# The 32 sample rows as weights in four column quarters, and the channel panels over 512 tokens twice

## The chip, the cores and the metric

The kernel runs on one core of a Trainium2 chip. The time is the device time of one launch in microseconds (us); the median of three timed runs of the kernel before is 4745.81 us (4744.82 to 4746.95). The profile is one further execution. The engines are named as in the profile: PE is TensorE's matmuls and PEld its weight loads, DVE is VectorE, ACT is ScalarE, POOL is GpSimd, SP is SyncE, which here only issues DMAs.

## The reference, cut to what matters

One step of a hybrid encoder layer for 1024 prompt frames and 32 sample frames: a combined input projection, differential attention, a causal convolution and a grouped state-space scan, output products, a retrieval over 16384 experts, and a gated per-layer embedding. The change lies in the combined projection, which is computed for both groups of frames with the same weights:

```python
h = rms_norm(x, lp['norm_mix_g'])
q, k, v, z, xbc, dt_raw, gates = jnp.split(h @ lp['w_in'], SPLIT_AT, axis=-1)
```

`h` is 1056 x 1024 here (1024 prompt rows, then 32 sample rows), and `w_in` is 1024 x 10272. All inputs are float32.

## The kernel before

`project_convolve_scan` is the first stage; attention and the retrieval follow it, each behind a barrier. It keeps h transposed on chip, so that the 1024 model channels lie on the partitions in 8 slices of 128. To get close to float32 from the faster `fp32r` matmuls, h and the weights are each held as a leading part and a rest, and `product` (line 94) makes three matmuls for each of the 8 slices: 24 in one unit of work. A matmul on plain float32 operands is issued as two instructions (two passes); the profile counts these.

The columns of `w_in` are cut into 27 panels: panel 0 is 512 columns of q; panels 1 to 6 are the 3072 channels of x, B and C ("xbc"); 7 to 10 are z; 11 and 12 are v; then 14 half panels of 256 columns follow, 6 of q and k and 8 of the gates. The panels of q, k, xbc and gates are "by channel": a block of 128 weight columns is the stationary operand, and the 1056 tokens stream in three units of `TS` = 352. There are 56 such blocks (4, then 24, then 28). The panels of z and v are "by token": 128 tokens are stationary and 512 weight columns stream; each has 9 units, and the ninth holds the 32 sample rows. After panel 0 comes the step size "dt" (32 columns), for 9 token tiles of 24 matmuls each.

What sets the order is written out by hand, and all engines are in program order:

- POOL loads panel p into the single raw buffer `wp` (`load`, line 310), which is free once DVE has split panel p-1. In POOL's own program the load of panel p+1 stands behind `keep_tail` and `put_past` (lines 323 and 315) for the four blocks of panel p-1, and the last of these waits until DVE has convolved the last block but one buffer ago.
- DVE splits a panel into lead and rest (lines 89 and 91), then convolves the four blocks of the panel before (lines 554 and 557). In the front part it scales and splits the transposed tiles of h and the four quarters of panel 0 (`scale`, `rest`, `first_panel`).
- PE computes the units into PSUM banks, six before the half panels and three (`NBS`) in them, and transposes each convolved block after the third unit of the next (line 937), when ACT has activated it (line 796).
- ACT moves each unit out of PSUM (line 767, and 784 for xbc), into one of four staging buffers, which SP stores.
- Beside the half panels the scan runs in 36 steps. Before each even unit PE does the step's sums (lines 1010 to 1012), before each odd one the products of the step before (1029 and 1030); DVE, ACT and POOL work between them. Three steps stand beside each half panel of six units. The steps' state rows are written out beside the first and the last of them.

## Time and profile before

| | |
|---|---|
| median of the timed runs | 4745.81 us |
| time of the profiled execution | 4760.91 us |
| its span | 4759.3 us |
| PE busy | 3775.6 us, 79% of the span |
| DVE busy | 2834.1 us, 60% |
| ACT busy | 1627.9 us, 34% |
| POOL busy | 1464.9 us, 31% |
| mean granted TensorE clock | 0.897 |
| the 24 matmuls of all `product` units at 128x352 into the low banks (lines 99 to 101) | 359.0, 329.4 and 329.0 us busy |

The span is from the first to the last instruction of the profiled execution; the time of that execution is 1.6 us more, and it lies 15 us above the median of the timed runs. Busy times of PE count each matmul from its start to its end, and matmuls overlap, so a matmul's cost is read from the distance between two starts. The first stage ends at about 1280 us. The granted clock is given as a share of 2.4 GHz.

### The profile page before, as it was taken

The numbers are of one execution on the slowest core, as the hardware profiler recorded it, in microseconds if no ns is written. First come the engines' busy times: TensorE is split into PE (matmuls) and PEld (weight loads), VectorE is DVE, ScalarE is ACT, GpSimd is POOL, SyncE is SP. The second block draws the span as 40 slices with busy tenths as digits, with TensorE's granted clock in tenths as the row PEclk, the third lists the DMA queues.
The fourth block names the chain that finished last, engine by engine and source line by source line (L and its number), as shares of the span: only waits on it lengthen the run. The fifth ranks groups of instructions, "written<-read, shape, count | busy, mean of one in ns | idle before, by whom it ended". The sixth has DMA issues, their size and how long they took to land.

```text
span 4759.3 us, 53107 instructions
## 1 busy us (share of the span) xinstructions
PE 3775.6 (79%) x17205; PEld 2215.6 (47%) x17205; DVE 2834.1 (60%) x6237; ACT 1627.9 (34%) x4726; POOL 1464.9 (31%) x1391
## 2 busy tenths in 40 slices
PE   8999999999899888867777878656765766666658
PEld 8999777888766674334232334311311212212212
DVE  3444113666377537666557666666766666666774
ACT  2222111234266302333333333334444344444433
POOL 1100002222111003334334444344444444444442
PEclk8999999999899999998888999877887878978879
DMA  2223222344323359999999999999999999999996
GB/s 93 74 84 124 88 90 73 125 129 129 110 81 102 109 184 373 403 402 395 387 377 380 408 405 419 420 419 416 411 419 407 407 419 411 399 421 418 416 404 266
DMA packets 310588, 1379.97 MB, mean 290 GB/s; under 512 B 37840, under 2 KB 112320, under 8 KB 175168
## 3 DMA queue, kind: packets, MB, share of 16 engines
q0 software_dynamic: 167728, 1166.48, 60.6%
q1 hardware_dynamic: 142608, 210.36, 12.7%
q8 instruction: 130, 2.13, 0.2%
q14 instruction: 122, 1.00, 0.1%
HBM read 1295.71 MB, written 81.01 MB: 289 GB/s over the span
## 4 chain that ended last, share of the span: by engine, by line
DMA 29%; PE 20%; DVE 7%; issue 4%; POOL 4%; ACT 2%; ACTq 0%; DVEq 0%; POOLq 0%
DMA peer_uv<-in_peer_uv_dram,peer_idx 29%; PE peer_acc L2762 10%; PE peer_fo L2701 4%; POOL peer_uv L1872 3%; DVE peer_uv L2018 3%; PE peer_fo L2714 2%; PE peer_fo L2601 2%; PE peer_tb L2545 1%; ACT peer_scaled L2336 1%; DVE peer_hot L1979 0%; DVE peer_hot L1982 0%; DVE peer_sel L1985 0%; ACT peer_ge L2331 0%; PE peer_acc L2650 0%; PE peer_fo L2619 0%
## 5 line engine op out<-in xcount | busy, mean ns | idle before, releaser
L2762 PE MATMUL peer_acc<-peer_uv,peer_scaled 128*64 128x512 f32 (+1 forms) x4224 | 1298.7, 734 | 699.3 <-ACT peer_scaled L2336 676.6
L2018 DVE CUSTOM_DVE_ANT_0 peer_uv<-peer_uv,peer_rep 128x1024 f32<-128x1024 f32 x1056 | 1282.8, 1224 | 938.0 <-DMA peer_uv<-in_peer_uv_dram,peer_idx 894.2
L1872 POOL DMA_INDIRECT peer_uv<-in_peer_uv_dram,peer_idx x1056 | 1217.6, 1153 | 1722.3 <-PE peer_acc L2762 1472.7
L2762 PEld LDWEIGHTS peer_acc<-peer_uv,peer_scaled 128*64 128x64 f32 (+1 forms) x4224 | 310.0, 158 | 1528.6 <-ACT peer_scaled L2336 953.4
L2331 ACT ACTIVATE peer_ge<-peer_pre 128x1 f32<-128x1 f32 x1056 | 213.4, 202 | 1678.3 <-DVE peer_pre L2018 1631.0
L2701 PE MATMUL peer_fo<-peer_space 128*128 128x256 f32 (+2 forms) x1152 | 407.4, 496 | 101.5 <-DVE peer_space L2072 44.1
L2336 ACT ACTIVATE peer_scaled<-peer_eased,peer_ge 128x64 f32<-128x64 f32 (+1 forms) x1056 | 366.4, 347 | 122.0 <-ACT peer_ge L2331 2.4
L99 PE MATMUL proj_bank<-proj_hTh,proj_wplead 128*128 128x352 f32 x1008 | 359.0, 356 | 1.8 <-DVE proj_wprest L91 1.8
L2329 ACT ACTIVATE peer_eased<-peer_fold,peer_gw 128x64 f32<-128x64 f32 (+1 forms) x1056 | 351.1, 332 | 1.1 <-DVE peer_gw L2000 1.1
L2701 PEld LDWEIGHTS peer_fo<-peer_space 128*128 128x128 f32 x1152 | 217.3, 201 | 285.9 <-issue 234.6
L100 PE MATMUL proj_bank<-proj_hTr,proj_wplead 128*128 128x352 f32 x1008 | 329.4, 327 | 0.0
L101 PE MATMUL proj_bank<-proj_hTh,proj_wprest 128*128 128x352 f32 x1008 | 329.0, 326 | 0.0
L767 ACT ACTIVATE proj_stg<-proj_bank 128x352 f32<-128x352 f32 (+2 forms) x117 | 57.7, 495 | 490.0 <-PE proj_bank L101 490.0
L99 PEld LDWEIGHTS proj_bank<-proj_hTh,proj_wplead 128*128 128x128 f32 x1008 | 193.7, 192 | 25.1 <-issue 22.2
L100 PEld LDWEIGHTS proj_bank<-proj_hTr,proj_wplead 128*128 128x128 f32 x1008 | 193.6, 192 | 15.9 <-issue 15.9
L101 PEld LDWEIGHTS proj_bank<-proj_hTh,proj_wprest 128*128 128x128 f32 x1008 | 193.1, 192 | 0.0
L89 DVE CAST proj_wplead<-proj_wp 128x4096 fp32r<-128x4096 f32 (+2 forms) x17 | 31.5, 1852 | 261.1 <-DMA proj_wp<-in_w_in_dram 126.4
L2714 PE MATMUL peer_fo<-peer_space 128*128 128x128 f32 (+1 forms) x1152 | 151.0, 287 | 38.6 <-DVE peer_space L2082 18.8
L2714 PEld LDWEIGHTS peer_fo<-peer_space 128*128 128x128 f32 (+1 forms) x1152 | 138.1, 189 | 85.3 <-issue 80.4
L2545 PEld LDWEIGHTS peer_tb<-peer_hT,peer_wq 128*128 128x128 f32 x1152 | 142.2, 202 | 69.3 <-issue 66.4
L2545 PE MATMUL peer_tb<-peer_hT,peer_wq 128*128 128x128 f32 x1152 | 155.0, 291 | 1.4 <-ACT peer_hT L2294 1.4
L1234 DVE CUSTOM_DVE_ANT_0 attn_e<-attn_S,bias_negdist 128x128 f32<-128x128 f32 (+5 forms) x144 | 103.1, 750 | 60.4 <-PE attn_S L1361 52.4
(376 smaller groups left out, 5460.6 us busy)
## 6 DMA issues: line engine op xcount, KB each, us to landing
proj_wp<-in_w_in_dram POOLq DMA_DIRECT2D x13, 2048.0 KB, 9.6
peer_space<-in_w_ssm_o_dram SPq DMA_DIRECT2D x48, 512.0 KB
peer_uv<-in_peer_uv_dram,peer_idx POOLq DMA_INDIRECT x1056
proj_wp<-in_w_in_dram POOLq DMA_DIRECT2D x14, 1024.0 KB, 7.9
peer_space<-in_w_attn_o_dram SPq DMA_DIRECT2D x24, 512.0 KB
peer_space<-in_w_out_dram SPq DMA_DIRECT2D x24, 512.0 KB
scratch_xtok<-proj_shared SPq DMA_DIRECT2D x20, 512.0 KB, 3.2
scratch_chan<-proj_stg SPq DMA_DIRECT2D x48, 176.0 KB
```

The lines of the kernel that those rows point to most:

```text
L99: pe.matmul(out, a.bitcast(F32R), b.bitcast(F32R), start=(k == 0), stop=False)
L100: pe.matmul(out, a.bitcast(F32R), br.bitcast(F32R), start=False, stop=False)
L101: mm = pe.matmul(out, ar.bitcast(F32R), b.bitcast(F32R), start=False, stop=(k == last))
L1872: pool.indirect_dma_start(uv[k][:], None, io["peer_uv"], bass.IndirectOffsetOnAxis(ap=idx[t % 2][:, col:col + 1], axis=0)).then_inc(uv_in[ ...
L2018: dve.tensor_tensor_reduce(uv[k][:, 0:D], uv[k][:, 0:D], rep[j][:], 1.0, 0.0, ALU.mult, ALU.add, pre[:, k:k + 1]).then_inc(u_done, 1)
L2329: act.activation(eased[n % 2][:, 0:r], fold[:] if r == DEC else fold2[:], ACT.Copy, scale=gw[t % 2][:, col:col + 1]).then_inc(eased_done, 1)
L2331: act.activation(ge[:, k:k + 1], pre[:, k:k + 1], ACT.Gelu_apprx_tanh).then_inc(gelu_done, 1)
L2336: act.activation(scaled[k][:, 0:r], eased[n % 2][:, 0:r], ACT.Copy, scale=ge[:, k:k + 1]).then_inc(scaled_done, 1)
L2545: x = pe.matmul(tb[h // 4][:, h % 4, :], wq[:, k, h * P:(h + 1) * P], hT[:, k, :], start=(k == 0), stop=(k == DK - 1))
L2701: x = pe.matmul(bank[n % 2][:, 0:e], w[q % WR][:, k, :], xb[p % 2][:, k, 0:e], start=(k == 0), stop=(k == CB - 1))
L2714: x = pe.matmul(bank[n % 2][0:r, i * P:(i + 1) * P], sm[:, k, inside(i, r)], w[q % WR][:, k, :], start=(k == 0), stop=(k == CB - 1))
L2762: x = pe.matmul(acc[group(t, slot % groups_of(t)), h:h + HALF], scaled[slot][:, 0:r], uv[slot][:, D + h:D + h + HALF], start=(it == 0 and ...
```

## The change

The 32 sample rows leave the three-matmul units. Their transposed h is kept in a buffer of its own in plain float32 (`own`) and is now the stationary operand, 32 columns wide; the raw float32 panel streams past it. The 8 slices of the contraction are dealt over four column quarters of the array, so that quarter q sums slices q and q+4 in rows 32q to 32q+31 of one PSUM bank (`quarters`). ACT copies the bank to `part`, and a matmul with `fold` (four 32x32 identities on top of each other) adds the four quarters up: by channel it gives 128 channels x 32 tokens with `part` as weights, by token 32 x 512 with `fold` as weights. Panel 0, whose raw buffer is needed early, uses its lead and rest instead. The step size is computed in the same way, with the 32 columns of its weights stationary.

The third unit of a channel block and the ninth of a token panel thus become one float32 matmul each, and the other two units of a channel block cover 512 tokens. In the half panels the two short units now stand behind the four long ones. PSUM gives up a bank for `quarters`, so the bank counts fall to 5 and 2, and the staging buffers to 3. Two waits are added on POOL's loads, since PE now reads the raw panel too. The sample part of panel p+1 stands on PE behind the first unit of panel p.

```diff
-TS = T // NSPLIT
+SEG = 512
...
-    NB, NBS, NST = 6, 3, 4
+    NB, NBS, NST = 5, 2, 3
...
+            blocks = PANELS[p][3] // P
+            order = [(a, b) for a in range(blocks) for b in range(NSPLIT)]
+            if p >= WIDE:
+                order = [x for x in order if x[1] < NSPLIT - 1] + [x for x in order if x[1] == NSPLIT - 1]
+            return [(FIRST[p] + u, a, b) for u, (a, b) in enumerate(order)]
...
+    def third(b):
+
+        return slice(b * SEG, min((b + 1) * SEG, T))
+
+    def third_width(b):
+        return third(b).stop - third(b).start
+
+    def part_at(p):
+
+        return p + NSPLIT if p else 0
...
-        wdth, wdtr = s.sb("wdth", [P, DK, SH]), s.sb("wdtr", [P, DK, SH])
+        own = s.sb("own", [P, DK, DEC])
         stg = [s.sb(f"stg{i}", [P, PANEL]) for i in range(NST)]
+        part, fold = s.sb("part", [P, PANEL]), s.sb("fold", [P, DEC])
...
+                    if p > 1:
+                        pool.wait_ge(part_made, part_at(p - 1 if p <= WIDE else p - 2) + 1)
                     pool.dma_start(raw_of(p), w_cols(col + at, w)).then_inc(panel_in[p % 2], 16)
...
+                dve.tensor_reduce(fold[:], c.ident[:].rearrange("p (q m) -> p m q", m=DEC), AX_X, ALU.add).then_inc(fold_done, 1)
...
+                def evacuate_part(p):
+                    w = PANELS[p][3]
+                    act.wait_ge(part_made, part_at(p) + 1)
+                    act.activation(part[:, 0:w], quarters[:, 0:w], ACT.Copy).then_inc(part_out, 1)
...
                 def evacuate_dt():
+                    for b in range(NSPLIT):
+                        act.wait_ge(part_made, b + 2)
+                        act.activation(part[:, 0:third_width(b)], quarters[:, 0:third_width(b)], ACT.Copy).then_inc(part_out, 1)
...
                 for p in range(1, len(PANELS)):
+                    evacuate_part(p)
                     if PANELS[p][0] != "xbc":
...
+                def sample_part(p):
+
+                    w = PANELS[p][3]
+                    if p:
+                        pe.wait_ge(panel_in[p % 2], 16 * (p // 2 + 1))
+                        pe.wait_ge(part_out, part_at(p))
+                    else:
+                        pe.wait_ge(h_lead, 2 * NT)
+                    terms = [(k, x) for k in range(0, DK, 4) for x in ((raw_of(p),) if p else (lead_of(p), rest_of(p)))]
+                    for i, (k, x) in enumerate(terms):
+                        for q in range(4):
+                            mm = pe.matmul(quarters[q * DEC:(q + 1) * DEC, 0:w], own[:, k + q, :], x[:, k + q, :],
+                                           start=(i == 0), stop=(i == len(terms) - 1))
+                    mm.then_inc(part_made, 1)
+
...
+                    w = third_width(b)
+                    pe.wait_ge(part_out, b + 1)
+                    terms = [(k, x) for k in range(0, DK, 4) for x in ((hTh[:, :, third(b)], hTr[:, :, third(b)]) if b < NSPLIT - 1 else (own[:],))]
+                    for i, (k, x) in enumerate(terms):
+                        for q in range(4):
+                            mm = pe.matmul(quarters[q * SH:(q + 1) * SH, 0:w], wdt[:, k + q, :], x[:, k + q, :],
+                                           start=(i == 0), stop=(i == len(terms) - 1))
+                    mm.then_inc(part_made, 1)
...
-                    if kind in BY_CHANNEL:
-                        cols, toks = slice(a * P, (a + 1) * P), slice(b * TS, (b + 1) * TS)
-                        mm = product(pe, bank[bank_of(n)][:, 0:TS], [(lead[:, k, cols], rest[:, k, cols]) for k in range(DK)],
+                    if kind not in BY_CHANNEL and a == NPT:
+                        pe.wait_ge(part_out, part_at(p) + 1)
+                        mm = pe.matmul(bank[bank_of(n)][0:DEC, :], fold[:], part[:], start=True, stop=True)
+                    elif kind in BY_CHANNEL and b == NSPLIT - 1:
+                        pe.wait_ge(part_out, part_at(p) + 1)
+                        if n < FIRST[1]:
+                            pe.wait_ge(fold_done, 1)
+                        mm = pe.matmul(bank[bank_of(n)][:, 0:DEC], part[:, a * P:(a + 1) * P], fold[:], start=True, stop=True)
+                    elif kind in BY_CHANNEL:
+                        cols, toks = slice(a * P, (a + 1) * P), third(b)
+                        mm = product(pe, bank[bank_of(n)][:, 0:SEG], [(lead[:, k, cols], rest[:, k, cols]) for k in range(DK)],
                                      [(hTh[:, k, toks], hTr[:, k, toks]) for k in range(DK)])
...
-                            pe.wait_ge(h_rest, 2 * 3)
+                            pe.wait_ge(h_rest, 2 * 4)
                     elif i == 4:
-                        pe.wait_ge(h_rest, 2 * 6)
-                    elif i == 8:
-                        pe.wait_ge(h_rest, 2 * NT)
+                        pe.wait_ge(h_rest, 2 * 8)
                     unit(0, n, a, b)
+                    if i == 6:
+                        sample_part(0)
...
-                for t in range(NT):
-                    n = rows_of(t)
-                    here = slice(t * P, t * P + n)
-                    mm = product(pe, bank[DT % NB][0:n, t * SH:(t + 1) * SH], [(hTh[:, k, here], hTr[:, k, here]) for k in range(DK)],
-                                 [(wdth[:, k, :], wdtr[:, k, :]) for k in range(DK)])
+                for b in range(NSPLIT):
+                    step_size_part(b)
+                    pe.wait_ge(part_out, b + 2)
+                    for t in range(4 * b, min(4 * b + 4, NT)):
+                        n, at = rows_of(t), (t - 4 * b) * P
+                        mm = pe.matmul(bank[DT % NB][0:n, t * SH:(t + 1) * SH], part[:, at:at + n], fold[:], start=True, stop=True)
...
+                sample_part(1)
...
                         unit(p, n, a, b)
+                        if i == 0 and p + 1 < len(PANELS):
+                            sample_part(p + 1)
```

Three places show what moves. The first is on PE, at the end of the first unit of panel 2 (`own` holds the sample rows, `wp` the raw panel, `tb` the transposes). Before:

```order
L101 MATMUL proj_bank<-proj_hTh,proj_wprest 128x352
L940 MATMUL proj_tb<-ident,proj_shared 32x128 [waits proj_rows_out]
L99 MATMUL proj_bank<-proj_hTh,proj_wplead 128x352 [waits proj_evac_done]
L100 MATMUL proj_bank<-proj_hTr,proj_wplead 128x352
L101 MATMUL proj_bank<-proj_hTh,proj_wprest 128x352
```

After:

```order
L101 MATMUL proj_bank<-proj_hTh,proj_wprest 128x512
L950 MATMUL proj_quarters<-proj_wp,proj_own 32x512 [waits proj_part_out,proj_panel_in1]
L950 MATMUL proj_quarters<-proj_wp,proj_own 32x512 x7
L1002 MATMUL proj_tb<-ident,proj_shared 32x128 [waits proj_rows_out]
L99 MATMUL proj_bank<-proj_hTh,proj_wplead 128x512 [waits proj_evac_done]
```

Eight float32 matmuls on the raw panel 3 stand between the first and the second unit of panel 2, and with them a wait for that panel's arrival.

The second place is on POOL: the load of panel 3 and what stands ahead of it in POOL's program, the last rows for the blocks of panel 1. Before:

```order
L326 COPY proj_tailr<-proj_shared 128x3
L320 COPY proj_shared<-proj_pastT 128x3 [waits proj_tail_kept,proj_convolved]
L326 COPY proj_tailr<-proj_shared 128x3 [waits proj_evac_done]
L326 COPY proj_tailr<-proj_shared 128x3
L320 COPY proj_shared<-proj_pastT 128x3 [waits proj_tail_kept,proj_convolved]
L313 DMA proj_wp<-in_w_in_dram 128x8x512 [waits proj_w_split]
```

After:

```order
L345 COPY proj_tailr<-proj_shared 128x3
L339 COPY proj_shared<-proj_pastT 128x3 [waits proj_tail_kept,proj_convolved]
L345 COPY proj_tailr<-proj_shared 128x3 [waits proj_evac_done]
L345 COPY proj_tailr<-proj_shared 128x3
L339 COPY proj_shared<-proj_pastT 128x3 [waits proj_tail_kept,proj_convolved]
L332 DMA proj_wp<-in_w_in_dram 128x8x512 [waits proj_part_made,proj_w_split]
```

The load stays where it was, with one wait more.

The third place is on PE in the half panels, at the third scan step of a panel (`scan` and `shared` hold the scan's tables, `seg`, `yh` and `tb` are its PSUM banks). Before, a unit of 24 matmuls follows the sums and another follows the products; one step's sums and the start of that unit are:

```order
L1010 MATMUL proj_seg<-proj_scan,below 128x512
L1011 MATMUL proj_yh<-proj_shared 128x128
L1012 MATMUL proj_tb<-proj_shared 128x512
L99 MATMUL proj_bank<-proj_hTh,proj_wplead 128x352 [waits proj_evac_done]
L100 MATMUL proj_bank<-proj_hTr,proj_wplead 128x352
```

After, from the third step's sums to the next panel's:

```order
L1075 MATMUL proj_seg<-proj_scan,below 128x512
L1076 MATMUL proj_yh<-proj_shared 128x128
L1077 MATMUL proj_tb<-proj_shared 128x512
L978 MATMUL proj_bank<-proj_fold,proj_part 128x32 [waits proj_part_out,proj_evac_done]
L1094 MATMUL proj_tb<-proj_scan 128x64 [waits proj_y_step,proj_cbm_done,proj_sadd_done,proj_wx_done,proj_out_done,proj_dtx_done,proj_M_done]
L1094 MATMUL proj_tb<-proj_scan 128x64 x7
L1095 MATMUL proj_yh<-proj_scan,proj_shared 128x512
L978 MATMUL proj_bank<-proj_fold,proj_part 128x32 [waits proj_part_out,proj_evac_done]
L1075 MATMUL proj_seg<-proj_scan,below 128x512 [waits proj_exp_done,proj_carried_done,proj_ld_in0,proj_sadd_done,proj_R_done,proj_w_split]
```

Between these sums and products, and between these products and the next sums, one matmul stands where 24 stood.

## Rows read from the trace of the kernel before

**Rows 1.** The profile page: busy time of each engine, share of the span, instructions.
```profile
PE 3775.6 (79%) x17205; PEld 2215.6 (47%) x17205; DVE 2834.1 (60%) x6237; ACT 1627.9 (34%) x4726; POOL 1464.9 (31%) x1391
```

**Rows 2.** Windows: stretch, its us, busy us of each engine, PEclk, DMA share, GB/s.
```profile
81.45:120.19 38.74, 38.74 (x218) 38.74 (x216) 0.00 (x0) 0.47 (x1) 0.00 (x0) 0.55 0.01 5
170.44:395.52 225.08, 209.27 (x1300) 206.88 (x1298) 103.33 (x73) 58.81 (x129) 18.04 (x53) 0.95 0.26 84
```

**Rows 3.** Timeline of PE: start us, us, engine, line, op; first matmuls of units.
```profile
58.41 0.32 PE L99 MATMUL proj_bank<-proj_hTh,proj_wplead 128*128 128x352 f32 x1
62.25 0.32 PE L99 MATMUL proj_bank<-proj_hTh,proj_wplead 128*128 128x352 f32 x1
...
557.95 0.39 PE L99 MATMUL proj_seg<-proj_wplead,proj_hTh 128*128 128x512 f32 x1
...
561.44 0.39 PE L99 MATMUL proj_seg<-proj_wplead,proj_hTh 128*128 128x512 f32 x1
```

**Rows 4.** Timeline of PE in the scan: products of one step, first matmuls after them.
```profile
1002.26 0.73 PE L99 MATMUL proj_bank<-proj_hTh,proj_wplead 128*128 128x352 f32 x1
...
1013.15 1.89 PE L1029 MATMUL proj_tb<-proj_scan 128*128 128x64 f32 x16
...
1015.39 0.73 PE L99 MATMUL proj_bank<-proj_hTh,proj_wplead 128*128 128x352 f32 x1
```

**Rows 5.** Timeline of PE in the retrieval: eight passes in two column halves, then in one quarter.
```profile
3114.62 1.94 PE L2762 MATMUL peer_acc<-peer_uv,peer_scaled 128*64 128x512 f32 x8 [1.52 <-ACT peer_scaled L2336]
...
4698.81 3.62 PE L2762 MATMUL peer_acc<-peer_uv,peer_scaled 128*32 128x512 f32 x8
```

**Rows 6.** Timeline of PE: from a product with 32 weight columns to one with 128.
```profile
748.89 1.02 PE L1012 MATMUL proj_tb<-proj_shared 128*32 128x512 f32 x2
749.85 0.43 PE L99 MATMUL proj_bank<-proj_hTh,proj_wplead 128*128 128x352 f32 x1
```

**Rows 7.** Timeline: PE's last transposes of panel 1 and first matmul of panel 2.
```profile
169.65 1.03 PE L937 MATMUL proj_tb<-ident,proj_shared 128*128 128x128 f32 x8
170.44 0.41 PE L99 MATMUL proj_bank<-proj_hTh,proj_wplead 128*128 128x352 f32 x1
```

**Rows 8.** Timeline of POOL: issue of the load of panel 3.
```profile
175.61 0.88 POOL L313 DMA_DIRECT2D proj_wp<-in_w_in_dram  x1
```

**Rows 9.** Timeline of DVE: splits of panels 3, 7 and 8, idle time before, releaser.
```profile
185.92 2.29 DVE L89 CAST proj_wplead<-proj_wp 128x4096 fp32r<-128x4096 f32 x1 [10.61 <-DMA proj_wp<-in_w_in_dram]
...
412.76 2.29 DVE L89 CAST proj_wplead<-proj_wp 128x4096 fp32r<-128x4096 f32 x1 [12.36 <-DMA proj_wp<-in_w_in_dram]
452.68 2.29 DVE L89 CAST proj_wplead<-proj_wp 128x4096 fp32r<-128x4096 f32 x1 [4.19 <-DMA proj_wp<-in_w_in_dram]
```

**Rows 10.** Waits of DVE from 100 to 460 us: us in total, times, longest.
```profile
DVE proj_wplead L89 <- DMA proj_wp<-in_w_in_dram: 126.4, 7, 66.9
```

**Rows 11.** Waits of PE from 0 to 440 us: us in total, times, longest.
```profile
PE proj_tb L937 <- ACT proj_shared L796: 15.8, 4, 4.9
```

**Rows 12.** Timeline of the front part: PE, DVE and ACT.
```profile
28.49 0.66 PE L99 MATMUL proj_bank<-proj_hTh,proj_wplead 128*128 128x352 f32 x1 [1.82 <-DVE proj_wprest L91]
...
33.53 0.69 DVE L89 CAST proj_wplead<-proj_wp 128x1024 fp32r<-128x1024 f32 x1
...
49.05 1.03 PE L908 MATMUL proj_tb<-ident,proj_shared 128*128 128x128 f32 x8
...
51.08 1.29 DVE L527 TENSOR_TENSOR proj_hTr<-proj_shared,proj_hTh 128x512 fp32r<-128x512 f32 x2
...
53.86 0.68 PE L908 MATMUL proj_tb<-ident,proj_shared 32*128 32x32 f32 x8
...
55.12 1.16 ACT L767 ACTIVATE proj_stg<-proj_bank 128x352 f32<-128x352 f32 x3
```

**Rows 13.** Timeline of DVE in a scan step: after the products, up to the next tables.
```profile
1002.86 0.69 DVE L664 TENSOR_TENSOR proj_shared<-proj_shared,proj_yh 128x512 f32<-128x512 f32 x1 [3.86 <-PE proj_yh L1030]
...
1007.51 0.68 DVE L685 TENSOR_TENSOR proj_scan<-proj_shared,dt 128x512 f32<-128x512 f32 x1
```

More of the change, by code:

```diff
@@ L167, in units @@
         if PANELS[p][0] in BY_CHANNEL:
-            return [(FIRST[p] + u, u // NSPLIT, u % NSPLIT) for u in range(UNITS[p])]
+            blocks = PANELS[p][3] // P
[3 more added lines that the diff above has]
+            return [(FIRST[p] + u, a, b) for u, (a, b) in enumerate(order)]
         return [(FIRST[p] + u, u, 0) for u in range(UNITS[p])]
@@ L256, in project_convolve_scan @@
                                 for x in (wph, wpr))
-        low = [s.ps(f"bank{i}", [P, PANEL]) for i in range(NBS)]
+        low, quarters = [s.ps(f"bank{i}", [P, PANEL]) for i in range(NBS)], s.ps("quarters", [P, PANEL])
         seg, yh = s.ps("seg", [P, 2 * PANEL]), s.ps("yh", [P, PANEL])
@@ L281, in project_convolve_scan @@
         ss_init, ss_done, ms_done, rr_done, xn_done = (s.sem(n) for n in ("ss_init", "ss_done", "ms_done", "rr_done", "xn_done"))
-        turned, scaled, h_lead, h_rest, wdt_split = (s.sem(n) for n in ("turned", "scaled", "h_lead", "h_rest", "wdt_split"))
+        turned, scaled, h_lead, h_rest = (s.sem(n) for n in ("turned", "scaled", "h_lead", "h_rest"))
         panel_in, w_split, quarter_split = s.sems("panel_in", 2), s.sem("w_split"), s.sem("quarter_split")
         mm_done, evac_done, stored = s.sem("mm_done"), s.sem("evac_done"), s.sems("stored", NST)
+        fold_done, part_made, part_out = s.sem("fold_done"), s.sem("part_made"), s.sem("part_out")
         taps_turned, taps_out, zeroed, past_put = (s.sem(n) for n in ("taps_turned", "taps_out", "zeroed", "past_put"))
@@ L398, in store @@
                         row = at + a * P
-                        dst, src = dr["chan" if kind == "qk" else "gT"][row:row + P, b * TS:(b + 1) * TS], stg[m % NST][:, 0:TS]
+                        dst, src = dr["chan" if kind == "qk" else "gT"][row:row + P, third(b)], stg[m % NST][:, 0:third_width(b)]
                     else:
@@ L569, in _ @@
                         scale(t - 2, 1)
-                        rest(t - 2, 0)
-                        rest(t - 2, 1)
+                        if t - 2 < NPT:
+                            rest(t - 2, 0)
+                            rest(t - 2, 1)
                     for quarter in {4: (0, 1), 5: (2,), 6: (3,)}.get(t, ()):
                         first_panel(quarter)
-                dve.wait_ge(wdt_in, 16)
-                split(dve, wdt, wdth[:], wdtr[:], wdt_split, 1)
                 panel(1)
@@ L756, in lead, with evacuate @@
                     act.wait_ge(scaled, k + 1)
-                    act.activation(hTh[:, 4 * h:4 * h + 4, t * P:t * P + n].bitcast(F32R), hc[h][:, :, 0:n], ACT.Copy).then_inc(h_lead, 1)
-                def evacuate(p, n, a):
+                    x = hTh[:, 4 * h:4 * h + 4, t * P:t * P + n].bitcast(F32R) if t < NPT else own[:, 4 * h:4 * h + 4, :]
+                    act.activation(x, hc[h][:, :, 0:n], ACT.Copy).then_inc(h_lead, 1)
+                def evacuate_part(p):
+                    w = PANELS[p][3]
+                    act.wait_ge(part_made, part_at(p) + 1)
+                    act.activation(part[:, 0:w], quarters[:, 0:w], ACT.Copy).then_inc(part_out, 1)
+                def evacuate(p, n, a, b):
                     kind = PANELS[p][0]
                     m = staged(n)
-                    r, w = (P, TS) if kind in BY_CHANNEL else (rows_of(a), PANEL)
+                    r, w = (P, third_width(b)) if kind in BY_CHANNEL else (rows_of(a), PANEL)
                     act.wait_ge(mm_done, n + 1)
@@ L781, in evacuate_xbc @@
                         act.wait_ge(tail_kept, 2 * (blk - 1))
-                    at = PRE + sl * TS
-                    w = min(TS, SEQ - sl * TS)
-                    y = act.activation(dst[:, at:at + w], x[:, 0:w], ACT.Copy)
-                    if w < TS:
-                        y = act.activation(dst[:, S0 + PRE:LEN], x[:, w:TS], ACT.Copy)
-                    y.then_inc(evac_done, 1)
+                    at = PRE + sl * SEG if sl < NSPLIT - 1 else S0 + PRE
+                    w = third_width(sl)
+                    act.activation(dst[:, at:at + w], x[:, 0:w], ACT.Copy).then_inc(evac_done, 1)
                 def activate(blk):
@@ L815, in _ @@
                         lead(t - 2, 1)
-                for n, a, _ in units(0):
-                    evacuate(0, n, a)
+                for i, (n, a, b) in enumerate(units(0)):
+                    if i == 7:
+                        evacuate_part(0)
+                    evacuate(0, n, a, b)
                 evacuate_dt()
@@ L862, in _ @@
                 for p in range(1, len(PANELS)):
+                    evacuate_part(p)
                     if PANELS[p][0] != "xbc":
-                        for i, (n, a, _) in enumerate(units(p)):
+                        for i, (n, a, b) in enumerate(units(p)):
                             j = n - BESIDE
@@ L868, in _ @@
                                 exps(u)
-                            evacuate(p, n, a)
+                            evacuate(p, n, a, b)
                             if j >= 0 and j % 2:
```

3 lines of the change are left out of this document (2 added, 1 removed).

## The prediction

> **What bounds the kernel now.** I read the page's busy times first: PE leads with 79% of the span, DVE has 60% [rows 1]. An average doesn't say whether PE bounds the stage that changes, so I looked at it next in windows, and it does: in the step-size stretch PE is busy for all of its 38.74 us at a granted clock of 0.55, and in the xbc panels 2 to 5 it is busy for 209.27 of 225.08 us [rows 2]. What is taken from PE's stream there comes off the end of the stage; the later stages stand behind a barrier and are the same work. Then I took the price of one unit, start to start: 24 matmuls over 352 columns take 62.25 - 58.41 = 3.84 us, and 15 over 512 take 3.49, so 24 take 5.58 [rows 3]. Both are 10.9 ns a column for the 24: weight loads are covered and columns are what is paid. Last I looked at what the new wait would wait for: the panel loads.
>
> **The sum, part by part** (minus is faster).
>
> The columns of a channel block fall from 1056 to 1024: 3 x 3.84 = 11.52 becomes 2 x 5.58 = 11.16. The block gains a fold: two passes with 128 weight columns. Sixteen such passes with 64 columns streamed take 1.89 us with the last one's latency, 0.11 each at most [rows 4], so 0.22. Net -0.14 a block; for the 52 blocks outside panel 0, -7.3 us.
>
> A token panel loses its ninth unit, 5.58. Its fold is two passes over 512 columns; eight passes in one quarter take 3.62 us, 0.43 each without the last one's latency [rows 5], so 0.86. Going between 32 and 128 weight columns costs about 0.1: after L1012's start at 748.89 two passes end at 749.75, and the next starts at 749.85 [rows 6]. Net -4.5; six panels, -27.1.
>
> A sample part is 8 float32 matmuls, 16 passes. The trace has no four quarters side by side. One quarter alone pays 0.43 a pass; two halves with separate outputs do eight passes in 1.94 us, four times 0.43 and a latency, so they run together [rows 5]. The bounds for 16 passes are 1.72 us (all four together) and 6.88 (one after the other), with 3.44 for two at a time. I take 1.72, the nearest mechanism being the two halves, and 0.2 for the two changes of shape: 1.92. Half panels stream 256 columns: 1.06. Parts 1 to 12 cost 12 x 1.92 = 23.0, parts 13 to 26 cost 14 x 1.06 = 14.8.
>
> The step size loses 38.74 [rows 2]. New are twice 16 float32 matmuls over 512 (3.44 each, four together), 8 over 32 columns (about 0.5), 9 folds (2.0) and three drains, in each of which PE waits for a copy by ACT of at most 0.6 plus its hand-over, 0.9: 12.1 in all. Net -26.6. Nothing else runs there that could hide the drains.
>
> Panel 0 gets dearer. Its first unit needs four token tiles instead of three. DVE finishes the fourth just before 33.53, where its next quarter split starts, while the unit started at 28.49: +5.0 [rows 12]. The fifth unit now needs tile 7, whose transposes come directly ahead: after those at 49.05 DVE's rest ended at 52.37, 3.3 us later, of which 0.8 is PE's own: +2.5 [rows 12]. The sixth unit now waits for the first evacuation (five banks), and ACT evacuates only behind all leads: 55.12 is 1.26 after the last transposes began at 53.86, plus 0.6 for the copy, less 0.6 of PE's own: +1.3 [rows 12]. Panel 0's sample part has lead and rest: 3.44 + 0.2; columns and folds give -0.6. Together +11.8.
>
> The new wait. The sample part of panel p+1 stands behind the first unit of panel p. Panel 2 starts at 170.44 [rows 7]; the load of panel 3 is issued at 175.61 [rows 8], 5.2 later, since POOL first waits for DVE to convolve the last block of panel 1; it arrives at 185.92, when DVE, idle since 175.31, starts its split [rows 9]. PE is there 5.58 after the panel's start and waits until 15.5. This repeats in panels 2 to 6. DVE's seven waits for loads sum to 126.4 [rows 10]; the first is the 66.9, the last 4.19 [rows 9]; the five left average 11.06, so arrivals average 4.87 + 11.06 = 15.9 after the panel's start. PE waits 10.3 each, 51 in all with a little off for the shorter last unit. Behind the waiting matmul are all units of the panel, and behind those ACT, DVE's next convolution and POOL's next load: the next panel shifts by the same amount and nothing catches up. Ahead of panel 8's split DVE is idle only 4.19, 6.9 less than that average [rows 9], so in panel 7 the arrival is some 9 to 10 after the start: +4. In panel 1 the load is issued with the panel's start; landing between 8 and 10.3 puts the wait between 3 and 5: +3. Later panels have their data early: there the load follows the split directly. Sum +58.
>
> Against that, PE's present waits for ACT's activation go, 15.8 in four panels [rows 11]: DVE's split and convolution run while PE waits for the load. Behind these waits matmuls ran slower: of the 225.08 us, 48 x 3.84 = 184.3 are units, 15.8 waits, and about 1.0 a block transposes (0.79 of it at 169.65 [rows 7]), which leaves 9.3, at a granted clock of 0.95 [rows 2]: 2.3 for each wait. Seven waits cost 16 then, 9.3 go: +7.
>
> The scan. Its period is 13.13 us a step [rows 4]. In every third step one fold stands between sums and products, and one between products and the next sums. The products then wait for DVE's small product on the sums (about 0.3), and the next sums for the state sum, DVE's first operation after the products (0.69 [rows 13]) less the 0.2 of the fold. DVE is ready with the tables: from 1002.86 to 1008.1, 5.3 us after the products [rows 13], just within a long unit's 5.58. I take 0.85 for each of 12 panels: +10; the bounds are 0 and a full 5 us of DVE's chain, +60.
>
> Sum: -7.3 - 27.1 + 23.0 + 14.8 - 26.6 + 11.8 + 58 - 15.8 + 7 + 10 = +48. On the profiled execution's 4760.9 that is 4809; on the median of the timed runs, 15 lower, 4794.
>
> The rows show two column halves at 3.62/1.94, close to twice as fast as one quarter [rows 5]. The Trainium skill, "TensorEngine Tiling (Array Packing)", section Key Properties, says that tiles work in parallel and that changing the mode drains the engine; the trace agrees with the first in halves. "TensorE: Matmul & The Clock Gate", section Measured speedup vs the span model, has 2.38 for three column tiles, 0.79 of the ideal; as an estimate by that page the quarter parts would cost a quarter more, some 11 us in all, and the time would be 4805.
>
> **Rivals.** (a) The quarters don't run together. For four in a row the trace has no evidence, against it the two halves [rows 5]. Serial passes add 5.16 to each of 12 wide parts, 2.58 to each of 14 half ones, 10.3 in panel 0 and 20.6 in the step size: +129, 4923. Two at a time add a third of that, +43: 4837. That is the rival in which the change doesn't do what it says.
> (b) The load wait doesn't count: the 58 are mostly given back, because the panel has arrived when PE reaches it, or because what PE loses is time that it had to wait for DVE anyway. Only the 15.8 is known as such. Without waits and their slow clock, but with the old ones gone, it is 48 - 58 - 16 = -26 and 4720; if only the old waits' time is exchanged, 48 - 58 + 15.8 - 7 = -1 and 4745. It is faster if the load of panel p+1 arrives less than 5.58 after the start of panel p; the issue alone comes after 5.2 [rows 7, 8].
> (c) The short third scan step costs DVE's whole chain, 3 to 5 us in each of 12 panels: +26 to +50 more, 4820 to 4844. For it speaks how close 5.3 is to 5.58; against it, that DVE is idle 3.86 before the products' end [rows 13].
>
> **Chances and range.** Forecast 0.68, own range 4775 to 4815; (a) 0.10; (c) 0.09; (b) 0.13, divided between no change and faster. About 9.5 us, 0.2%, is what a measurement tells from no change. Slower by more: 0.68 + 0.10 + 0.09 = 0.87 less a little for the forecast's lower tail, 0.85. Within: 0.08; faster: 0.07. The range 4765 to 4845 takes in the two-at-a-time case and most of (c), and leaves out serial quarters and real gains.
>
> **What would show it.** In the profile after: PE waiting for the DMA of the raw panel at L950, seven times, about 10 us in panels 2 to 6; eight float32 matmuls at L950 within 1.9 us; the step size in 12 us; the waits for the activation gone; the scan's panel period at 41 us instead of 3 x 13.13 = 39.4; the first unit at 33.5. I am wrong if those waits are short, if the sample parts take over 3 us, or if the scan's period passes 43.

## The result, and the profile after

The changed kernel takes 4828.84 us (median of 4 runs, 4826.27 to 4835.32) against 4746.38 before: ratio 1.0174, 95% interval 1.0158 to 1.0191. That is 82 us slower. The forecast was 4794 with a range of 4765 to 4845: the sign and the range held, the size was 35 us short, and the narrow range of 4775 to 4815 was missed. The span of the profiled execution is 4825.4 us.

The program of the later stages did not change. Attention's first matmul starts at 1294.37 us before and at 1375.29 after, 80.9 later, which is about the 82 of the medians; so the loss is looked for ahead of it. (Behind it the two traces differ the other way: 3464.9 us before, 3450.1 after. The profiled execution before lies 15 us above its median. In the traces of the other kernels that stretch takes 3450 to 3462, so single traces tell the later stages apart no better than that, and what follows compares attention's start.) The page and the windows after, which answer to [rows 1] and [rows 2] (stretch, its us, busy us and instructions of each engine, granted clock, DMA share, GB/s):

```profile
PE 3777.6 (78%) x16171; PEld 2051.7 (43%) x16171; DVE 2832.7 (59%) x6234; ACT 1635.7 (34%) x4732; POOL 1471.7 (30%) x1391
```

```profile
92.68:104.49 11.81, 9.81 (x100) 4.17 (x99) 0.00 (x0) 1.80 (x7) 0.00 (x0) 1.00 0.10 29
169.57:439.19 269.62, 215.59 (x1010) 166.38 (x1009) 103.69 (x73) 58.33 (x117) 20.22 (x53) 0.94 0.22 68
243.10:250.60 7.50, 0.21 (x1) 0.00 (x0) 0.00 (x0) 0.60 (x1) 0.01 (x1) 0.72 0.78 280
250.60:254.20 3.60, 3.55 (x16) 0.59 (x16) 3.47 (x2) 0.00 (x0) 0.00 (x0) 0.50 0.02 5
```

PE issues a thousand instructions fewer and is busy for as long as before, so the page alone shows nothing. The windows do: the step size fell from 38.74 us to 11.81, and the xbc panels 2 to 5, the same four panels as in [rows 2], grew from 225.08 us to 269.62 although PE is busy for only 6 us more in them. The rest is idle time. The last two lines are one load wait (PE idle for 7.3 of the 7.50) and the sample part behind it, at a granted clock of 0.50, which is the 1.2 GHz level.

The waits of PE in the first stage, answering to [rows 11] (us in total, times, longest):

```profile
PE proj_quarters L950 <- DMA proj_wp<-in_w_in_dram: 45.6, 7, 7.7
PE proj_tb L999 <- ACT proj_shared L821: 31.9, 20, 3.0
...
PE proj_bank L99 <- DVE proj_hTr L547: 7.1, 1, 7.1
PE proj_seg L1075 <- DVE proj_shared L683: 5.9, 8, 0.8
PE proj_tb L1094 <- DVE proj_scan L711: 5.9, 1, 5.9
PE proj_tb L1094 <- issue: 5.4, 11, 0.6
```

The first is the forecast load wait, seven times. The second was forecast to vanish (15.8 us, four times, before); it doubled, and it now comes in 20 of the blocks, 19 times with 1.52 us and once, in panel 1, with 3.04. The timeline of one block of panel 3 shows what it is (start us, us, engine, line, operation, out<-in; in brackets the idle time ahead and its releaser):

```profile
260.95 0.30 PE L978 MATMUL proj_yh<-proj_fold,proj_part 128*128 128x32 f32 x2
261.15 0.60 ACT L812 ACTIVATE proj_shared<-proj_seg 128x512 f32<-128x512 f32 x1 [6.23 <-PE proj_seg L101]
261.64 1.08 ACT L821 ACTIVATE proj_shared<-proj_shared 128x1059 f32<-128x1059 f32 x1
262.62 0.19 ACT L812 ACTIVATE proj_shared<-proj_yh 128x32 f32<-128x32 f32 x1
...
262.77 1.09 PE L999 MATMUL proj_tb<-ident,proj_shared 128*128 128x128 f32 x8 [1.52 <-ACT proj_shared L821]
262.84 0.83 DVE L574 TENSOR_SCALAR proj_shared<-proj_shared,proj_tapsT 128x1059 f32<-128x1059 f32 x1 [5.39 <-ACT proj_shared L812]
```

ACT does the activation of the last block (L821) behind the copy of this block's second third, as its program has it. PE needs it after this block's third unit. That unit was 24 matmuls, 3.84 us [rows 3]; now it is a fold of 0.14 us. So ACT's copy and activation, 1.7 us together, lie open, and PE idles for 1.5 of them. DVE isn't the cause: it had been idle for 5.39 us when it started its next convolution.

Where the 80.9 us are, from the starts of the panels in both traces:

| stretch | before | after | difference | forecast |
|---|---|---|---|---|
| start to panel 1 | 120.5 | 106.7 | -13.9 | -12.9 |
| panel 1 | 49.9 | 62.9 | +13.0 | +6.7 |
| panels 2 to 5 | 225.1 | 269.6 | +44.5 | +30.3 |
| panel 6 | 47.3 | 59.9 | +12.6 | +13.9 |
| panel 7 | 50.3 | 56.2 | +5.8 | +3.7 |
| panels 8 to 12 | 255.1 | 242.5 | -12.6 | -13.8 |
| half panels, to attention | 546.1 | 577.5 | +31.4 | +19.9 |

The last column divides the prediction's own terms among the stretches (its 16 us of slow clock as 2.3 for each wait). Panel 1 and panels 2 to 5 miss by 20 us together, the half panels by 11; each of the others is within about 2.

### The profile page after: what moved, and what is told of

The parts are those of the page before. It is cut to its first block, busy times and chain, and to the rows that moved or that the text cites. A ratio compares the mean times of both kernels' runs of the same rounds, so it can differ in the third digit from the quotient of the medians.

```text
span 4825.4 us, 51155 instructions
## 1 busy us (share of the span) xinstructions
PE 3777.6 (78%) x16171; PEld 2051.7 (43%) x16171; DVE 2832.7 (59%) x6234; ACT 1635.7 (34%) x4732; POOL 1471.7 (30%) x1391
## 3 DMA queue, kind: packets, MB, share of 16 engines
q1 hardware_dynamic: 142608, 210.36, 12.6%
## 4 chain that ended last, share of the span: by engine, by line
DMA 29%; PE 19%; DVE 7%; issue 4%; POOL 4%; ACT 1%; ACTq 0%; DVEq 0%; POOLq 0%
DMA peer_uv<-in_peer_uv_dram,peer_idx 29%; PE peer_acc L2829 10%; PE peer_fo L2768 4%; POOL peer_uv L1939 3%; DVE peer_uv L2085 3%; PE peer_fo L2668 2%; PE peer_fo L2781 2%; PE peer_tb L2612 1%; ACT peer_scaled L2403 1%; DVE peer_hot L2049 0%; DVE peer_hot L2046 0%; DVE peer_sel L2052 0%; PE peer_acc L2717 0%; ACT peer_ge L2398 0%; PE peer_fo L2686 0%
## 5 line engine op out<-in xcount | busy, mean ns | idle before, releaser
L99 PE MATMUL proj_bank<-proj_hTh,proj_wplead 128*128 128x512 f32 x624 | 266.4, 427 | 8.7 <-DVE proj_hTr L547 7.1
L101 PE MATMUL proj_bank<-proj_hTh,proj_wprest 128*128 128x512 f32 x624 | 248.6, 398 | 0.0
L100 PE MATMUL proj_bank<-proj_hTr,proj_wplead 128*128 128x512 f32 x624 | 245.9, 394 | 0.0
L792 ACT ACTIVATE proj_stg<-proj_bank 128x512 f32<-128x512 f32 (+2 forms) x112 | 54.6, 490 | 458.4 <-PE proj_bank L101 425.0
L99 PEld LDWEIGHTS proj_bank<-proj_hTh,proj_wplead 128*128 128x128 f32 x624 | 118.8, 190 | 49.6 <-issue 23.3
L100 PEld LDWEIGHTS proj_bank<-proj_hTr,proj_wplead 128*128 128x128 f32 x624 | 118.7, 190 | 35.8 <-issue 10.1
L101 PEld LDWEIGHTS proj_bank<-proj_hTh,proj_wprest 128*128 128x128 f32 x624 | 118.3, 190 | 26.3
```

Source lines behind the costliest of these rows:

```text
L99: pe.matmul(out, a.bitcast(F32R), b.bitcast(F32R), start=(k == 0), stop=False)
L100: pe.matmul(out, a.bitcast(F32R), br.bitcast(F32R), start=False, stop=False)
L101: mm = pe.matmul(out, ar.bitcast(F32R), b.bitcast(F32R), start=False, stop=(k == last))
```

## The experiments

Ten kernels ran, in three groups; each group has its own runs of the kernel before on the same chip (medians 4748.5, 4751.3 and 4747.9).

**The load wait: a later sample part.**

```diff
-                        if i == 0 and p + 1 < len(PANELS):
+                        if i == (6 if p <= XLAST + 1 else 0) and p + 1 < len(PANELS):
                             sample_part(p + 1)
```

> The changed kernel, with the sample part of the next panel issued behind the seventh unit of a panel instead of behind the first, in panels 1 to 7. Theory A (PE's 45.6 us of waits for the load are lost time, and each leaves some 2.8 us of slow clock behind it): 65 us go, from 4829; since DVE still waits for the load ahead of its split and only then convolves the first block of the panel, an activation comes 2 to 4 us late in five panels, 10 to 20 us come back: 4775 to 4785. Rival (the load's wait only stands in for waits that PE has anyway, so that it is exchanged for them): at most 15 us faster, 4814 or more.

Measured: 4773.07 us, ratio to before 1.0055 (1.0039 to 1.0072); 56 below the changed kernel, and 56.8 earlier at attention's start (1318.49). No wait for a load is left in the first stage. The part takes its short time again, here in panel 2:

```profile
200.14 1.92 PE L950 MATMUL proj_quarters<-proj_wp,proj_own 128*32 128x512 f32 x16
```

Theory A holds: the waits are lost time. They were 45.6 us. The seven parts took 23.8 us in place of 7 x 1.855 = 13.0, and the units behind them 44.3 in place of 39.3: 15.8 us more at the low clock. Of these 61.4, 4.6 came back; the waits for the activation grew by 1.7 of that (31.9 to 33.6). The expectation had 10 to 20 coming back through DVE's convolution, so its 4775 to 4785 lies slightly too high.

**The activation: one place earlier in ACT's order.**

```diff
-                        if sl == 1 and blk:
+                        if sl == 0 and blk:
                             activate(blk - 1)
```

> The changed kernel, with ACT's activation of a block issued behind the copy of the next block's first third instead of its second. Theory A (ACT's order: the activation stands behind the copy of the second long unit, which now ends only 0.14 us ahead of the transposes instead of a unit): the 31.9 us of PE's waits for the activation go, 1.7 in each of 20 blocks, 4797. Rival (DVE's convolution is what is late, through its wait for the load and its split): no change, 4829.

Measured: 4798.51 us, ratio 1.0108 (1.0091 to 1.0125), and attention starts 31.8 us earlier (1343.49). No wait at L999 is left; the load waits are 48.3. The same block of panel 3:

```profile
240.63 1.07 ACT L821 ACTIVATE proj_shared<-proj_shared 128x1059 f32<-128x1059 f32 x1
...
246.03 0.42 PEld L978 LDWEIGHTS proj_yh<-proj_fold,proj_part 128*128 128x128 f32 x2
246.26 0.30 PE L978 MATMUL proj_yh<-proj_fold,proj_part 128*128 128x32 f32 x2
246.29 0.94 PEld L999 LDWEIGHTS proj_tb<-ident,proj_shared 128*128 128x128 f32 x8
246.40 1.07 PE L999 MATMUL proj_tb<-ident,proj_shared 128*128 128x128 f32 x8
```

The activation is done 4.6 us ahead of the transposes, which follow the fold at once. Theory A holds: nothing was late but ACT's place in its own order. That the gain (31.8 by the traces, 30 by the medians) equals the 31.9 of the waits so closely is partly luck, since the load waits grew by 2.7 us.

**Both, and DVE's first convolution ahead of its split.** Besides the two edits above:

```diff
+                    if XFIRST + 1 <= p <= XLAST + 1:
+                        convolve(4 * (p - 1 - XFIRST))
                     if p <= WIDE:
                         panel(p)
```

(and the loop that follows starts one block later).

> The changed kernel with the late sample part, the early activation, and DVE convolving the first block of a panel ahead of its split of the next panel's weights. Theory A: both waits and the slow clock behind them go, 45.6 + 19.6 + 31.9 = 97 us, 4732, which is below the kernel before. Rival (one bound stands behind the others, so that the gains do not add): 4765 to 4790.

Measured: 4729.38 us, ratio 0.9964 (0.995 to 0.9978). The gains add: 99 us off the changed kernel by the medians and 95.7 by attention's start (1279.55), 97 forecast; the two single edits gave 56.8 and 31.8, and the 7 us beyond them were not divided further. Through the xbc panels PE never waits:

```profile
146.40:400.00 253.60, 253.60 (x1253) 202.59 (x1252) 129.16 (x90) 71.29 (x142) 35.20 (x65) 1.00 0.30 95
```

With the three orders mended the change would have been measured as a small gain. Whether it is the quarters' gain is settled further down.

**The scan: short units apart.** The line that puts the folds of a half panel at its end is taken out (long, long, short, twice).

```diff
-            if p >= WIDE:
-                order = [x for x in order if x[1] < NSPLIT - 1] + [x for x in order if x[1] == NSPLIT - 1]
```

> The changed kernel with the folds of the half panels left in their blocks (long, long, short, long, long, short) instead of both at the panel's end; nothing before the half panels changes. Theory A (the stalls of 2.5 us a panel beside the short units are hand-overs between two engines, each beside its own short unit): no gain, within 5 us of 4829. Rival (a whole scan step of 7.4 us is too short for what DVE and ACT do in one, and spreading the short units gives each step a long one): 1.5 to 2.5 us in each of 12 panels, 4799 to 4811.

Measured: 4822.44 us, ratio 1.0158 (1.0141 to 1.0175); attention starts 11.3 us earlier. The panel period in the scan's steady part is 41.64 us in both. So a short unit costs the same wherever it stands, as theory A had it, and the rival's gain in each panel isn't there. But the kernel gained 6 to 11 us all the same, which neither theory expected. Nearly all of it came from one place, the second half panel with scan steps: 53.57 us from sample part to sample part in the changed kernel, 43.18 here. The panel behind it gave another 3.0, and 2 went the other way elsewhere. In the changed kernel:

```profile
872.21 0.30 PE L978 MATMUL proj_bank<-proj_fold,proj_part 128*128 128x32 f32 x2
878.37 3.64 PE L1094 MATMUL proj_tb<-proj_scan 128*128 128x64 f32 x16 [5.86 <-DVE proj_scan L711]
881.81 2.02 PE L1095 MATMUL proj_yh<-proj_scan,proj_shared 128*128 128x512 f32 x2
883.62 0.47 PE L978 MATMUL proj_bank<-proj_fold,proj_part 128*128 128x32 f32 x2
885.41 1.09 PE L1105 MATMUL proj_tb<-ident,proj_shared 128*128 128x128 f32 x4 [1.32 <-DVE proj_shared L687]
```

```profile
877.17 0.69 DVE L711 COPY proj_scan<-proj_tb 128x512 f32<-128x512 f32 x1 [9.28 <-DMA out_dram<-proj_scan]
```

PE waits there for the copy of a state (L711), which itself waited 9.28 us for a store; with only short units around it the wait lies open, and the sixteen products take 3.64 us in place of 1.89 [rows 4]. From 872.1 to 897.2 the granted clock was 0.73. In the reordered kernel the copy still waited 7.3 us for a store, but PE waited only 0.5 for the copy. The kernel before had two such stalls in its early scan steps too (8.3 us of waits), so most of this is no loss against it: the second and third half panels took 94.4 us before, 99.8 in the changed kernel and 86.2 reordered.

**The same with the three mends, and the part as a cover.** One kernel has the three mends and the folds in their blocks; the next moves, besides, the half panels' sample part to where PE waits:

```diff
+                        if p >= WIDE and i == 2 and p + 1 < len(PANELS):
+                            sample_part(p + 1)
                         unit(p, n, a, b)
```

> The changed kernel with the three mends of the xbc panels and, besides, the folds of the half panels left in their blocks. Theory (the 10 us that this order gained before came from one place, the second scan panel, where two short units in a row left PE idle and its clock low): some 10 us off 4729, 4719. Rival (that gain came from being late against other engines, and is gone with the mends): 4729.

Measured: 4722.40 us, ratio 0.9942 (0.9925 to 0.996), with runs from 4711 to 4730. Attention starts at 1265.49 against 1279.55 in the kernel without the new order. The same panel gives 9.9 of these 14.1 (52.89 to 43.03), so the gain from the order stands with the mends; another 4.7 are one steady panel that took 46.33 us in the older trace, with a wait of 2.46 that the profile can't name, and are not the order's.

> The same, with the sample part of the next half panel issued in each half panel between the scan's sums and the first short unit, instead of behind the panel's first unit. Theory (the stall of 0.67 us between a short unit and the products behind it is a fixed hand-over, PE to DVE and back, into which the part's 1.0 us fits): 0.67 in each of 13 panels, 8 to 9 us below the other kernel of this pair, 4711. Rival (DVE is behind by its throughput, so that PE waits for it whatever stands in between, or the part's changes of shape cost what it covers): no difference, 4719.

Measured: 4707.80 us, ratio 0.9914 (0.9894 to 0.9935), 14.6 below its pair by the medians and 9.1 by attention's start (1256.41). The intervals of the two kernels overlap a little, so I go by the second, and by the period of a half panel: it falls from 41.64 to 41.00 us in every steady panel, 0.64 where 0.67 was forecast. In the changed kernel the short unit is followed by an open 0.6 (further down the same place stands with the part in it):

```profile
1012.19 0.30 PE L978 MATMUL proj_bank<-proj_fold,proj_part 128*128 128x32 f32 x2
1013.09 1.97 PE L1094 MATMUL proj_tb<-proj_scan 128*128 128x64 f32 x16 [0.59 <-issue]
1014.89 1.08 PE L1095 MATMUL proj_yh<-proj_scan,proj_shared 128*128 128x512 f32 x2
1015.81 0.30 PE L978 MATMUL proj_bank<-proj_fold,proj_part 128*128 128x32 f32 x2
1016.84 1.96 PE L1075 MATMUL proj_seg<-proj_scan,below 128*128 128x512 f32 x4 [0.73 <-DVE proj_shared L683]
```

The row says "issue", that is, nothing that the profile can name. DVE's small product on the sums, for which the program has the products wait, stands here:

```profile
1012.39 0.29 DVE L669 TENSOR_TENSOR proj_shared<-proj_yh,upper 128x128 f32<-128x128 f32 x1 [3.01 <-PE proj_tb L1077]
```

With the part in front of the fold:

```profile
921.27 1.07 PE L950 MATMUL proj_quarters<-proj_wp,proj_own 128*32 128x256 f32 x16
922.27 0.41 PE L978 MATMUL proj_bank<-proj_fold,proj_part 128*128 128x32 f32 x2
922.52 1.98 PE L1094 MATMUL proj_tb<-proj_scan 128*128 128x64 f32 x16
```

From fold to products it is 0.25 us instead of 0.90. The wait is gone because something else fills the time from the sums on. That fits a hand-over of fixed length, PE to DVE's small product and back, and speaks against DVE being behind in throughput; that it is this product and no other releaser is read from the program, not from a row.

**One part alone: the step size.** The kernel before with the step size in quarters, all panels as they were (channel panels over 3 x 352, token panels with nine units). The core of what it keeps of the change:

```diff
+                for b in range(NSPLIT):
+                    step_size_part(b)
+                    pe.wait_ge(part_out, b + 1)
+                    for t in range(4 * b, min(4 * b + 4, NT)):
...
+                        mm = pe.matmul(bank[DT % NB][0:n, ...], part[:, at:at + n], fold[:], start=True, stop=True)
```

> The kernel before with one part of the change, the step size in column quarters (weights of 32 columns, three parts, nine folds); its ring has five banks and three staging tiles, as in the changed kernel, all panels are as before. Theory (the parts of the change are independent, and this one is worth what the traces show, 38.74 us before and 11.8 after): 27 us off 4748, 4721. Rival (what PE saves there is handed back at the next wait for a load or an activation, since the panels behind it come earlier): 4735 or more.

Measured: 4730.19 us (4722.59 to 4730.88), ratio 0.9949 (0.9932 to 0.9966): 21 us by the medians, 28.0 by attention's start (1266.40). The median lies between the forecast 4721 and the rival's 4735 and doesn't decide. The trace does: panel 1 starts at 94.23 instead of 120.52, 26.3 earlier, and no wait takes it back; those for the activation went from 15.8 to 17.3 only. The gain is kept; the rival falls.

**The token panels as well.** `sample_part` and the fold for the panels of z and v alone.

> The same, and besides it the six token panels with their sample rows in column quarters and a fold instead of the ninth unit; the channel panels stay at three passes of 352 tokens. Theory (a token panel of the changed kernel took 47.82 us where the one before took 50.13): 2.3 us in each of six, 14 us off the kernel with the step size alone, 4707. Rival (the part is paid in full and only the fold is small, so that the ninth unit's 5.6 us come back as part, fold and changes of shape): 4721, no gain.

Measured: 4715.35 us, ratio 0.9923 (0.9906 to 0.9939): 15 us more by the medians, 10.5 by attention's start (1255.93); the rival had no gain. A token panel takes 47.82 us here too (468.13 to 515.95).

**And the two orders mended.** Early activation, and the first convolution ahead of the split, in that kernel.

> The same again, with ACT's activation behind the first third's copy and DVE convolving a panel's first block ahead of its split. Theory (the waits for the activation, 15.8 us before, and the slow clock behind them, 9.3, go): 25 us more, 4682. Rival (DVE's split now comes too late for the next panel or for the part): 4700 or more.

Measured: 4689.31 us (4684.4 to 4692.79), ratio 0.9864 (0.9848 to 0.9881); attention starts at 1229.35, 26.6 earlier than without the mends (25 forecast). It is the fastest of all, 1.4% below the kernel before.

**The mends without the change.** The kernel before with these two edits and nothing else.

> The kernel before with nothing of the change, and only the early activation and DVE's convolution of a panel's first block ahead of its split. It prices by itself what the changed kernel with all three mends gained that has nothing to do with the quarters. Theory: 15.8 us of waits and 9.3 of slow clock go, 4723, so that the full change with the same mends (4729) is no gain over it. Rival (before, the activation was not on the path): 4740 or more, and the full change keeps its lead.

Measured: 4727.62 us, ratio 0.9948 (0.9931 to 0.9964), attention's start 27.3 us earlier. It equals the mended full change (4729.38), and by attention's start (1267.10 against 1279.55) it is even ahead of it. The changed kernel's recovery to below the kernel before was therefore not the quarters': the mends alone bring as much. Which of the two edits does it here was not run apart.

The price of the quarters in the channel panels follows from two kernels with the same mends: with them attention starts at 1279.55, without them (step size and token panels still in quarters) at 1229.35. That is 50.2 us, or 36 with the better order of the half panels and 27 with the part as a cover. Of the 50.2, 13.5 lie ahead of panel 1, where the first unit has to wait for a fourth token tile and panel 0 has a part of its own, 4.6 from there to the half panels, and 32.1 in the half panels (4.7 of these are the one slow panel named above). So of the change's three parts two gain, 28 and 10 us, and the third, as it was written, loses what they gain and more; in the best order that ran it still costs 27.

## Why the prediction was right and where it fell short

The steps that held:

- **The quarters run together.** A sample part of 16 passes over 512 columns took 1.92 us in the profile; rival (a) is out. That the forecast has the same 1.92 is luck in the last digit: the row counts the last pass's latency, the forecast two changes of shape in its place (from the part's start to the next unit's it is 1.85). The step size came to 11.81 us (12.1 forecast).

```profile
561.08 1.92 PE L950 MATMUL proj_quarters<-proj_wp,proj_own 128*32 128x512 f32 x16
```

- The first unit began at 33.36 (33.5 forecast), the wait ahead of the fifth was 2.3 us (2.5), and panel 1 began 13.9 us earlier (12.9).

```profile
33.36 0.77 PE L99 MATMUL proj_bank<-proj_hTh,proj_wplead 128*128 128x512 f32 x1 [7.09 <-DVE proj_hTr L547]
```

- The token panels gained 2.3 us each with a wide part (2.6 forecast).
- **The load wait is real and little gives it back** (4.6 of 61.4 us), so rival (b) is out: the late part showed it.

The number alone would fit two rivals: 4829 lies in (c)'s 4820 to 4844 and near the 4837 of quarters that run two at a time. The traces exclude both, by the 1.92 us of a part and by the scan below.

The terms that were mis-sized:

- **"PE's present waits for ACT's activation go, 15.8 in four panels"** is the step that failed. They became 31.9, an error of 32 us. That is about the whole of the miss in size, but only because the other errors, -12, -4 and +14, nearly cancel, which is luck. I had reasoned from DVE, whose split and convolution made the old waits late, and I had priced the fold as 0.22 us of work. I did not ask what the 3.84 us unit that it replaced had been covering on ACT. The early activation took these waits away, all 31.9 us. What would be late next was worked out for DVE alone.
- The load waits: 45.6 in place of 58. The load of panel 4 is issued at 242.23, 4.75 after the panel's start (5.2 forecast), and PE, there at 243.1, waits until 250.6; in panels 2 to 6 I had taken an arrival 15.9 after the start from DVE's averages, and it was 13.1 to 13.5.

```profile
242.23 0.88 POOL L332 DMA_DIRECT2D proj_wp<-in_w_in_dram  x1 [0.32 <-issue]
```

- The slow clock: 15.8 us behind seven waits (16 forecast), of which 9.3 replaced what was there before. This held. Another 1.6 us, which no term had, came in the unit behind the one activation wait of 3.04.
- The scan: a panel takes 41.64 to 41.7 us where 41 was forecast. The stall beside the two short units is 1.7 us (0.85 forecast): before, a step's sums and products cost 13.13 - 2 x 3.84 = 5.45; the step with both short units runs from its sums at 1009.39 to the next at 1016.84, about 7.4 us, which is the 5.45, two folds of 0.14 and the stall. The place from 872 to 897, which I had not looked at, makes the two panels there 5.4 us dearer than before where some 3 were forecast. Rival (c), DVE's whole chain at 3 to 5 us in each panel, is out: the stall is smaller, spreading the short units changed no period, and a part put in front of the fold took 0.64 of it away.
- A fold costs 0.14 us, not 0.22: 4 us of gain over 52 blocks.

Balance, forecast to measured: 48 - 12.4 (load) + 31.9 (activation) - 4 (folds) + 14 (scan) = 77.5, against 80.9 in the traces; 1.6 of the rest is the slow unit in panel 1. The 14 is the part that is least well divided. It is what the half panels miss, 11.5, and the 2.2 that their folds saved; 10 of it are the stall in 12 panels, some 2 the place from 872 to 897.

Attention's start moved by 10.5 us and not 14 with the token panels in quarters, although the panels themselves gave the 14: the second and third half panels, where the state copy waits for a store, took 94.4 us in it and 90.3 in the kernel with the step size alone. That place differs by 4 us from kernel to kernel, so the 28 and the 10 are each known to about that, and their sum of 38 better. What stays open: what sets those waits for a store, and gains by the medians differ from those by attention's start by up to 7 us.

## What to carry to other kernels

A unit of work is also a cover. When one becomes short, list for every other engine what it did during that unit, in its program order, and see what now lies open; here a unit worth 3.84 us had hidden 1.7 us of ACT, and moving one line in ACT's order was worth 32 us. Split a change into its parts and price each alone: two parts of this one are worth 38 us together, and the third hides that. And give the mends that you find to the kernel before as well, or they are booked as the change's gain.

## What the runs showed of the hardware

- Four quarters of 32 weight columns, each with its own weights and its own moving data, pass 512 columns in about 0.43 us together, what one alone takes [rows 5]. In the step size, groups of eight passes start at 92.73, 93.61, 94.47 and 95.33 us, so two fours take 0.86 to 0.88, and 32 passes of panel 0's part took 3.57. That is 3.9 to 4 times one quarter. "TensorE: Matmul & The Clock Gate" of the Trainium skill, section Measured speedup vs the span model, has 2.38 for three column tiles, which is 0.79 of the ideal; no run here shows such a loss.
- The change between 32 and 128 weight columns shows as about 0.1 us each way (the units before and behind a part take 5.69 and 5.68, where 5.57 is usual).
- Behind five of the six waits of 5.5 us and more for a load the granted clock was 0.50 for the whole of the part, 3.57 us in place of 1.85, and the next unit took 0.5 to 1.1 more than its 5.62; behind the sixth it rose within the part (3.26 us, and no slow unit). The 19 waits of 1.52 left no slow matmul behind: the units after them took 5.62 us. The one of 3.04 did: the unit after it took 7.2.
- A fold of 32 streamed columns against 128 x 128 weights took 0.14 us for its two passes, less than the 0.11 a pass that sixteen passes of 64 columns had suggested.
